# An encoder trunk's attention stage rewritten: outputs with features on partitions, probabilities normalised before they are transposed, latent queries made feature-major

## The reference, cut to what matters

```python
q_a = apply_axial_rope(rms_norm(q_a, g_q_a), cos_a, sin_a)      # 8 heads of 64
k_a = apply_axial_rope(rms_norm(k_a, g_k_a), cos_a, sin_a)      # 2 kv heads
o_a = block_attention(q_a, k_a, v_a).reshape(b, s, WIDTH_A)
q_b = (rms_norm(c_q, g_cq) @ w_uq).reshape(b, s, N_HEADS_B, QK_NOPE_DIM + QK_ROPE_DIM)   # 64 + 32
q_rope = apply_axial_rope(q_rope, cos_b, sin_b)
kv = (rms_norm(c_kv, g_ckv) @ w_ukv).reshape(b, s, N_HEADS_B, QK_NOPE_DIM + V_DIM_B)
k_rope = apply_axial_rope(k_r, cos_b, sin_b)                    # shared by the 8 heads
o_b = block_attention(q_full, k_full, v_b).reshape(b, s, WIDTH_B)
o = jnp.concatenate([rms_norm(o_a, g_out_a), rms_norm(o_b, g_out_b)], axis=-1) @ w_o
x = x + gate_a * o
```

## Time and profile before

| what | us |
|---|---|
| median of 3 executions | 1194.02 (1192.86 to 1194.55) |
| the profiled execution, its own time | 1194.76 |
| its span, first to last instruction | 1193.0 |
| PE busy / weight loads | 1165.8 / 997.4 |
| DVE busy | 728.9 |
| POOL busy | 568.4 |
| ACT busy | 534.5 |
| the 32 pairs' maxima on DVE (L1758) | 39.2 |
| `ada` products of 1024 columns on DVE (L1387, 64 of them) | 89.1 |

### The profile page before, as it was taken

One profiled execution on the slowest core, in us unless ns is written; L12 is line 12 of the kernel. 1 busy time (PEld: TensorE's weight loads), 2 busy tenths in 40 slices (PEclk: granted clock), 3 DMA queues, 4 the chain that ended last, 5 costly groups with the idle time before them and its releaser, 6 DMA issues.

```text
span 1193.0 us, 18770 instructions
## 1 busy us (share of the span) xinstructions
PE 1165.8 (98%) x6288; PEld 997.4 (84%) x6288; DVE 728.9 (61%) x1481; ACT 534.5 (45%) x866; POOL 568.4 (48%) x768
## 2 busy tenths in 40 slices
PE   9999999999999999999999999999999999999997
PEld 6897887998888888888789979889888888888886
DVE  5878986767766677757666438746775134412345
ACT  5347675254431344234354677635543234422432
POOL 2487500655655445644665540054555544454462
PEclk9999997999999999999999999999999999999998
DMA  9743333423445444544433202222343322332322
GB/s 350 307 168 116 92 103 107 141 72 132 174 139 207 133 166 176 194 141 176 141 110 119 75 1 89 89 89 71 124 141 106 106 86 90 106 106 74 102 89 71
DMA packets 43979, 151.55 MB, mean 127 GB/s; under 512 B 5122, under 2 KB 7810, under 8 KB 43908
## 3 DMA queue, kind: packets, MB, share of 16 engines
q1 hardware_dynamic: 43908, 150.64, 36.6%
HBM read 148.52 MB, written 2.10 MB: 126 GB/s over the span
## 4 chain that ended last, share of the span: by engine, by line
PE 46%; issue 24%; POOL 15%; POOLq 6%; DVE 6%; DVEq 2%; ACT 1%; ACTq 0%
POOL w_lo L535 14%; PE ps L614 14%; PE ps L620 14%; PE ps L615 14%; POOLq L536 5%; DVE ada_prod L1387 2%; DVEq L1389 1%; DVE nmx L1758 1%; PE ps L749 1%; PE ps L950 1%; PE ps L738 1%; PE ps L718 0%; DVE ada_prod L1608 0%; DVE o_sb L1771 0%; PE ps L726 0%
## 5 line engine op out<-in xcount | busy, mean ns | idle before, releaser
L535 POOL TENSOR_TENSOR w_lo<-w_raw,w_hi 128x256 fp32r<-128x256 f32 x712 | 532.1, 779 | 599.3 <-ACT w_hi L1117 575.7
L614 PE MATMUL ps<-h_hi,w_hi 128*128 128x512 f32 (+1 forms) x960 | 349.7, 364 | 4.2 <-DVEq L1561 2.2
L615 PE MATMUL ps<-h_lo,w_hi 128*128 128x512 f32 (+1 forms) x960 | 347.3, 362 | 0.0
L620 PE MATMUL ps<-h_hi,w_lo 128*128 128x512 f32 (+1 forms) x960 | 347.2, 362 | 0.0
L1117 ACT CAST w_hi<-w_raw 128x1024 fp32r<-128x1024 f32 x178 | 183.2, 1047 | 183.8 <-PE ps L614 183.6
L614 PEld LDWEIGHTS ps<-h_hi,w_hi 128*128 128x128 f32 x960 | 181.7, 189 | 36.8 <-DVEq L1561 3.8
L1809 DVE SCALAR_TENSOR_TENSOR u_sb<-ps,par,u_sb 128x510 f32<-128x510 f32 x176 | 131.7, 748 | 123.2 <-ACT u_sb L1345 110.2
L620 PEld LDWEIGHTS ps<-h_hi,w_lo 128*128 128x128 f32 x960 | 181.7, 189 | 27.5
L615 PEld LDWEIGHTS ps<-h_lo,w_hi 128*128 128x128 f32 x960 | 181.8, 189 | 27.2
L614 PE MATMUL ps<-a_hi,w_hi 128*128 128x512 f32 (+1 forms) x400 | 146.6, 366 | 3.3 <-DVEq L1595 2.4
L620 PE MATMUL ps<-a_hi,w_lo 128*128 128x512 f32 (+1 forms) x400 | 145.6, 364 | 0.0
(11 more groups left out here) (160 smaller groups left out, 1372.6 us busy)
## 6 DMA issues: line engine op xcount, KB each, us to landing
w_raw<-w_slots SPq DMA_DIRECT2D x178, 512.0 KB, 3.5
ada_raw<-ada_slots SPq DMA_DIRECT2D x88, 512.0 KB, 3.8
shift<-shift_slots SPq DMA_DIRECT2D x8, 512.0 KB, 13.2
x_tok<-x_rows SPq DMA_DIRECT2D x4, 512.0 KB, 9.6
x<-x_t SPq DMA_DIRECT2D x4, 512.0 KB, 13.7
y_t<-x SPq DMA_DIRECT2D x3, 512.0 KB, 2.9
y_t<-x SPq DMA_DIRECT2D x1, 256.0 KB, 3.0
y_t<-x SPq DMA_DIRECT2D x2, 128.0 KB, 2.7
```

Source lines behind the costliest of these rows:

```text
L535: nc.gpsimd.tensor_tensor(w_lo[:, j, c], w_raw[:, j, c], w_hi[:, j, c].bitcast(F32), ALU.subtract)
L614: hh = mm(out, stat[0], mov[0], start=first, stop=False)
L615: hl = mm(out, stat[0], mov[1], start=False, stop=False)
L620: return mm(out, stat[1], mov[0], start=False, stop=last)
```

## The change

- **Outputs** swap their operands: the values (64 columns) are the weights, the transposed probabilities (256 columns) move; the two heads of a pair write to the two halves of the partitions (column halves of the array). `o_t` has features on partitions, so `output_transposes` goes.
- **Normalisation** moves ahead of the transposes: the `Exp` gives the row sums (`accum_out`), DVE takes the reciprocal and scales two of the four tiles, POOL the other two (`scale_rows`). The transposes of pair j move from step j+1 to step j+2, the outputs from j+2 to j+3.
- **Latent queries** are computed feature-major: 8 tiles of 512 columns (`qn`, four, scaled by ACT; `qr`, four, holding the rotary part and its swapped copy, multiplied on DVE by a table `tq`, which a new DMA of 128 KB loads). Scores of group B are two products of 64 rows for each head (latent part, rotary part), heads on row halves. The fills of group B, POOL's rotation and its copies of the keys go.
- **Copies**: the fills of group A, one value tile and the four key tiles move from ACT to DVE; the outputs are copied by DVE.
- **Norm of a group**: POOL squares and adds (`add_squares`), PE sums over partitions with a matrix of ones (`group_sums`, 512, 256 and 256 + 256 columns), ACT takes the root in PSUM, DVE the reciprocal in PSUM (`group_inverse`) and scales (`output_scaled`); group B is taken in two parts, one for each sequence. The output projection is cut into its group A half and its group B half.
- POOL's low parts of weight slots WO+1 to WO+3 are spread over steps 2 to 13, a quarter in each.
- One `ada` slot of layer 0 moves from behind the loop into the output projection.

```diff
--- before.py
+++ after.py
...
-                nc.gpsimd.tensor_tensor(qb[:, :, :, NOPE:], qb[:, :, :, NOPE:], qb_tmp[:], ALU.add)
-                nc.gpsimd.drain()
-                pool.wait_ge(krt_ready, L + 1)
-                nc.gpsimd.tensor_copy(kb_t[NOPE:QK_B, 1:, :], kb_t[NOPE:QK_B, 0:1, :].broadcast_to([ROT, HEADS - 1, T]))
...
+                def scale_rows(j):
+
+                    pool.wait_ge(rin_ready, NP * L + j + 1)
+                    for c in (2, 3):
+                        nc.gpsimd.tensor_scalar(prob[:, j % 2, c, :], prob[:, j % 2, c, :], rinv[:, j, c:c + 1], None,
+                                                ALU.mult)
+                    nc.gpsimd.drain()
+                    pool.sem_inc(second_scaled, 1)
...
+                def add_squares(j):
+
+                    group, s, _ = PAIRS[j]
+                    k, c = pair_tile(j), slice(s * SEQ, (s + 1) * SEQ)
+                    total = (ssum if group == "a" else ssq_b)[:, c]
+                    pool.wait_ge(o_done, NP * L + j + 1)
+                    if k % 4 == 0:
+                        nc.gpsimd.tensor_tensor(total, o_t[:, k, c], o_t[:, k, c], ALU.mult)
+                    else:
+                        nc.gpsimd.tensor_tensor(o_sq[:, 0, :], o_t[:, k, c], o_t[:, k, c], ALU.mult)
+                        nc.gpsimd.drain()
+                        nc.gpsimd.tensor_tensor(total, total, o_sq[:, 0, :], ALU.add)
+                    nc.gpsimd.drain()
+                    pool.sem_inc(o_summed, 1)
+
...
+                        n = L * SLOTS + S_WO + 1 + (i - 2) // 4
+                        lo_quarter(n % RING, n, (i - 2) % 4)
...
+                pe.wait_ge(ct_ready, 3 * L + 2)
+                for n in range(HEADS):
+                    j = slot(L, S_UQ + n // 4)
+                    key = ("uq", n)
+                    wait_free(pe, L, key)
+                    for k in range(2):
+                        at = (n % 4 * 2 + k) * P
+                        last = product(ps[:, bank(key), :], [r[:, j, at:at + P] for r in (w_hi, w_lo)],
+                                       [r[:, k, :] for r in (ct_hi, ct_lo)], k == 0, k == 1,
...
                     for q in range(2):
-                        for u in range(2):
-                            if group == "a":
+                        if group == "a":
+                            parts = [(q_t[:, j % 2, q * P:q * P + P], ka_t[:, c])]
+                        else:
...
+                            parts = [(qn[:, p, at:at + P], kn[:, p, c]), (qr[:, p, at:at + P], kr_t[:, c])]
+                        for n, (st, mv) in enumerate(parts):
+                            for u in range(2):
...
-                                st = q_t[0:QK_B, j % 2, u, q * P:q * P + P]
-                                mv = kb_t[0:QK_B, heads[u], s * SEQ:(s + 1) * SEQ]
-                            last = mm(ps[:, S_BANK[j % 2] + u, q * SEQ:(q + 1) * SEQ], st, mv, start=True, stop=True)
+                                last = mm(ps[:, S_BANK[j % 2] + u, q * SEQ:(q + 1) * SEQ], st[r], mv[r], start=n == 0,
+                                          stop=n == len(parts) - 1)
...
                     for u in range(2):
+                        if u == 1:
+                            pe.wait_ge(second_scaled, NP * L + j + 1)
                         for q in range(2):
-                            pe.wait_ge(exp_ready, 4 * (NP * L + j) + 2 * u + q + 1)
+                            if u == 0:
+                                pe.wait_ge(first_scaled, 2 * (NP * L + j) + q + 1)
...
-                    for u in range(2):
-                        for q in range(2):
-                            for k in range(2):
-                                v = va[:, 2 * s + k, u, :] if group == "a" else vb[:, 2 * s + k, heads[u], :]
-                                c = (2 * u + q) * VW
-                                last = mm(ps[:, O_BANK, c:c + VW], prob_t[:, j % 2, u, k, q * P:q * P + P], v,
-                                          start=(k == 0), stop=(k == 1))
+                    for k in range(2):
+                        for u in range(2):
+                            v = va[:, 2 * s + k, u, :] if group == "a" else vb[:, 2 * s + k, heads[u], :]
+                            last = mm(ps[64 * u:64 * u + 64, O_BANK, 0:SEQ], v, prob_t[:, j % 2, u, k, :],
+                                      start=(k == 0), stop=(k == 1))
                     last.then_inc(o_full, 1)
...
+                def group_sums(n):
...
+                    if n == 2:
+                        pe.wait_ge(last_sq, L + 1)
+                        last = mm(sum_view(n), ones[:], o_sq[:, 1, :], start=False, stop=True)
+                    last.then_inc(group_sum, 1)
+
...
+                for i in range(NP + 3):
...
+                        prob_transposes(i - 2)
+                    if 0 <= i - 3:
+                        outputs(i - 3) if i < NP + 2 else None
+                    if i == NA + 3:
+                        group_sums(0)
+                    if i == NP - 1:
+                        group_sums(1)
+                out_part(L, 0, (2, 3))
+                outputs(NP - 1)
+                out_part(L, 1, range(KD // 2))
+                group_sums(2)
                 for m in range(2, TAIL):
-                    out_tile(L, m, range(KD), 1)
+                    out_part(L, m, range(KD // 2))
+                for m in range(TAIL):
+                    out_part(L, m, range(KD // 2, KD), int(m > 0))
                 norm_tail(2 * L + 1, lambda m, s, release: half_out(L, m, s, release))
...
                         for c in range(4):
                             A(prob[:, i % 2, c, :], ps[:, S_BANK[i % 2] + c // 2, (c % 2) * SEQ:(c % 2 + 1) * SEQ],
-                              ACT.Exp, bias=nmx[:, i, c:c + 1]).then_inc(exp_ready, 1)
...
+                              ACT.Exp, bias=nmx[:, i, c:c + 1], accum_out=rsum[:, i, c:c + 1]).then_inc(exp_ready, 1)
...
+            def group_inverse(L, n):
+
+                dve.wait_ge(group_root, 3 * L + n + 1)
+                V.reciprocal(sum_view(n), sum_view(n))
...
+            def output_scaled(L, e):
+
+                k, c, _, _ = event(e)
+                V.scalar_tensor_tensor(out=o_t[:, k, c], in0=o_t[:, k, c], scalar=par[:, L, PC_GOUT + k:PC_GOUT + k + 1],
+                                       in1=sum_view(e // (KD // 2)), op0=ALU.mult, op1=ALU.mult).then_inc(on_ready, 1)
...
+                for p in range(HEADS // 2):
+                    key = ("uq", HEADS // 2 + p)
+                    wait_full(dve, L, key)
+                    V.tensor_tensor(halves(qr[:, p, :]), halves(ps[:, bank(key), :]),
+                                    tq[:].rearrange("p (o t) -> p o t", o=1).broadcast_to([P, NSEQ, SEQ]), ALU.mult)
+                    V.drain()
+                    dve.sem_inc(free[bank(key)], 1)
...
+                def take_keys(p):
+
+                    key = ("key", p)
+                    wait_full(dve, L, key)
+                    V.tensor_copy(kn[:, p, :], ps[:, bank(key), :])
...
+                def scale_rows(j):
+
+                    dve.wait_ge(exp_ready, 4 * (NP * L + j + 1))
+                    V.reciprocal(rinv[:, j, :], rsum[:, j, :])
+                    V.drain()
+                    dve.sem_inc(rin_ready, 1)
+                    for c in range(2):
+                        V.tensor_scalar(prob[:, j % 2, c, :], prob[:, j % 2, c, :], rinv[:, j, c:c + 1], None,
+                                        ALU.mult).then_inc(first_scaled, 1)
...
+                def take_outputs(j):
...
+                    dve.wait_ge(o_full, NP * L + j + 1)
+                    V.tensor_copy(o_t[:, k, c], o)
+                    V.drain()
+                    dve.sem_inc(o_done, 1)
...
+                take_fill(0)
+                for i in range(NP + 1):
+                    if i + 1 < NA:
+                        take_fill(i + 1)
                     if i < NP:
-                        b = S_BANK[i % 2]
-                        dve.wait_ge(s_full, NP * L + i + 1)
-                        V.tensor_reduce(out=nmx[:, i, :], in_=ps[:, b:b + 2, :].rearrange("p u (q k) -> p (u q) k", q=2),
-                                        op=ALU.max, axis=AX_X, negate=True).then_inc(max_ready, 1)
+                        maxima(i)
+                    if i == 0:
+                        take_values(3)
+                        take_keys(0)
+                    if i == 1:
+                        take_keys(1)
+                    if i >= 1:
+                        scale_rows(i - 1)
+                    if i == 1:
+                        take_keys(2)
+                    if i == 2:
+                        take_keys(3)
+                    if i < NP:
                         ada_step(L, i, 0)
...
-                for k in range(2, KD // 2):
-                    output_lo(L, k)
-                normalise_group(L, 1)
-                for k in range(KD // 2, KD):
-                    output_lo(L, k)
```

(75 more changed lines are left out.)

455 lines of the change are left out of this document (204 added, 251 removed).

## The result

After the change the kernel takes 1237.05 us (median of four runs, 1236.62 to 1242.15) where the kernel before takes 1193.44 beside it: 43.6 us more, ratio 1.0379, 95% interval 1.0346 to 1.0411. The forecast was 1221.5 in a range of 1204 to 1242. The profiled execution of after is the longest of the four, 1242.15 for a span of 1240.4, and stands 5.1 over their median. So stages are compared here from that mark on: from it to the end of the span before takes 1107.6 us, after 1153.1, which is 45.5 more.

What follows compares the result with a forecast made beforehand. The prediction took DVE, without slack and level with PE in layer 0 and layer 1's group B, as the bound. Layer 0 +20.2, layer 1 +7.0 and table load +0.3 gave +27.5: 1221.5 us, range 1204 to 1242.

Steps and rivals of the forecast that it cites:

- The mechanism that it named: Attention loops: DVE has no slack and paces, so its added work outweighs PE's savings; slower, 1221.5 us, chance 0.55.
- Layer 0's start: Up to layer 0's first maxima: ACT's latent 2.5 us later, four `qr` products 3.2, two fills 1.0; +6.7.
- Layer 0's loop: Layer 0's steps to the end of step 15: net DVE work +19.0 us, meetings with POOL +2.5.
- Layer 0's tail: Behind layer 0's step 15: DVE's list hidden under PE's, 36.0 us falling to 28.3, taken as -8.
- its twin in layer 1: Behind layer 1's last step: the tail falls from 31.3 to 28 us, -3.3.
- Layer 1: Layer 1's attention: start +3, group A -5, group B +12.3 (4.2 of it POOL), tail -3.3; together +7 us.
- the clock as the pace of the loop: Attention loops: PE, less busy, stays at the 1.2 GHz level; slower, +20, 1241 us, chance 0.15.
- POOL as the pace: Attention loops: POOL's stretched work makes steps about 6.3 us for 5.7; slower, +12, 1233 us, chance 0.12.
- PE still pacing, faster: Attention loops: DVE's additions stay small, so PE's -10.3 us a layer comes through; 1173.5 us, chance 0.10.
- The signs that were to be seen: Layer 0: DVE never idle, maxima to maxima 5.7 to 6.2 us, outputs about 1.06 a pair; tails of 28.
- `ada` at 1.5: DVE's `ada` products were to take 1.5 us on average, as a sign that the forecast was right.
- POOL the last releaser: Probability transposes on PE: POOL being the last they wait for was listed as a sign that the forecast was wrong.

Runs made afterwards that it cites:

- g1: Kernel before the change, with one unneeded DVE product of 1,024 columns added at the end of each of the 16 steps of both layers: 1224.14 us.
- e3: Kernel after the change, with the `ada` products inside the attention loops left out (zeros in their place): 1189.99 us.
- e4: Kernel after the change, with ACT instead of DVE copying query fills 2 to 7 and the outputs of pairs 0 to 13: 1230.02 us.
- e2: Kernel after the change, with POOL's two scalings of a pair left out and DVE's list unchanged: 1234.59 us.
- e6: Kernel after the change, with layer 0's two `ada` slots moved behind the first two fills, ahead of the first maxima: 1237.05 us.
- e5: Kernel after the change, with PE's sum of group B's first sequence moved from step 15 to step 16: 1233.86 us.
- e7: Kernel after the change, with the eight `ada` products beside layer 0's first four output tiles left out (zeros in their place): 1233.23 us.
- f2: Kernel after the change, with the three reciprocals of broadcast sums replaced by copies of the same width: 1234.05 us.
- e9: Kernel after the change, with twelve more 128x128 PE transposes in each of steps 3 to 17: 1244.56 us.
- f1: Kernel after the change; ACT copies fills and outputs and scales for DVE, PE's sum in step 16, two `ada` slots behind the fills: 1221.28 us.

## Why the prediction was right in direction and short in size

The mechanism that it named holds in layer 0's loop: DVE had no slack (g1), PE's saved work brought nothing, and what the change puts on DVE is paid (e3, e4). In layer 1's group B it holds with a part for POOL (e2). Point by point, in spans: 47.4 in all for +27.5. Of the missing 19.9 the tails and what follows the first make 13.0.

- **Ahead of the change**: 2.0 of the 47.4 lie in front of the rotary key, a start that wanders by up to 4.6 us. What moves it stays open.
- **Layer 0's start**, +6.7: measured 8.7 from the key on. The terms were right in kind (ACT's latent late by 2.5, four `qr`, two fills); left out were PE's gaps around them, because the fills stood behind four `ada` products (e6: 1.7) and the first scores came at the lower clock level (granted clock 0.50 from 113.70 to 115.80; 2.0 us for the eight records that took 1.06 before). Timeline of DVE:

```profile
112.55 0.42 DVE L1796 COPY q_t<-ps 128x256 f32<-128x256 f32 x1
113.78 0.42 DVE L1796 COPY q_t<-ps 128x256 f32<-128x256 f32 x1 [0.81 <-PE ps L926]
115.80 1.22 DVE L1804 TENSOR_REDUCE nmx<-ps 128x4 f32<-128x1024 f32 x1 [1.59 <-PE ps L955]
```

- **Layer 0's loop**, +19.0 + 2.5 = +21.5: measured 105.6 - 82.4 = +23.2, with two errors of opposite sign. Reciprocal and two scalings take (2.5 + 13.0 + 2.3) / 15 = 1.19 us a pair, for 0.8: +5.9. In exchange `ada` got shorter, 1.402 to 1.253 on average in this loop, where contention was to add; that is -4.8. Copies at 0.42 with 0.12 behind them, `group_inverse` 3.37 for 3.1, `output_scaled` 0.74 for 0.75 stood as forecast. The reciprocal went by the row: 6.6 ns an element, where the estimate from the Trainium skill (VectorE: DVE Perf Modes, First, the fixed hardware budget) was 4.3 us for 512; measured is 3.37.
- **Layer 0's tail**, 36.0 to 28.3, -8: measured 30.8, -5.2, and 6.2 given back behind it. This is the step that failed, with its twin in layer 1 (31.3 to 28, measured 32.0). It summed PE's list from the end of step 15 at the pace of a PE that had been busy. But the order of the sums let PE stand still for 7.9 and 6.8 us just ahead of it, and the same list then took 30.6: it starts at a granted clock of 0.50, and the first sums, eight transposes and eight output records take 1.9 us more than their later likes. Without that wait both tails are 3.7 and 3.5 shorter (e5). And a shorter tail outran POOL's splitting of the weights (e7: 5.3). A gain on PE was counted without asking who feeds it.
- **Layer 1**: start 2.8 for 3; group A -7.1 for -5; group B to the end of step 15 +15.0 for +12.3, of which POOL's scaling explains 4.1 (e2) and the inverse 3.5 (f2). The forecast had 4.2 for POOL, but as contention that makes DVE's instructions longer; measured, DVE's busy time there doesn't change with POOL's scaling, and the 4.1 are waits of DVE for PE and of PE for POOL. That the numbers agree is luck.
- **Rivals**: the clock as the pace of the loop is refuted (e9). Nor does PE stay low there, as that rival had it: layer 0's B in after holds transposes, scores, outputs and one sum, and its granted clock is 0.93. In the tails it costs some 2 us each (estimate from the rows behind PE's wait). POOL as the pace is refuted for layer 0 (e2), though PE's waits name it first; in layer 1 its scaling costs 6.0 us (e2), and in f1, with DVE relieved, it may cost more. That rival's 8.3 us a step is a slip, 3.8 times 2.28 is 8.7; its 6.3 and 1233 stand. PE still pacing, faster, is refuted by g1 on the kernel before and by the result. The signs that were to be seen: maxima to maxima 5.3 to 6.4 in the plain steps of layer 0, outputs 1.02 from the first to the next matmul at the full clock; `ada` at 1.5 was wrong, and "POOL the last releaser", meant as a sign against, was seen and proved nothing.

## What to carry to other kernels

Before taking work off the busiest engine, add a dummy instruction of known length to each other engine's loop: one run shows who has slack, stage by stage. The name at the end of a wait is the last to finish, and need not be the pace; leave its work out and see, stage by stage, whether the step gets shorter. Leaving out one engine's work can also shorten another's instructions, so look at every engine's busy time before you call it proof. When a stage shrinks on one engine, walk its suppliers: banks still held, weights still to be split, in the order in which the queues hold them.
